# Sliding-window attention inside the projection stage: other start slots for its steps, other slots for the K and V turns, and another order in the sample stage

## What is computed

```python
z = rms_norm(x, norm_g) @ w_in                      # q, k, v, gate | wq, wk, wv, wgate
# stick-breaking, per head
log_keep = where(mask, log_sigmoid(-z), 0)
after = cumsum(log_keep, reverse=True) - log_keep
o = where(mask, exp(log_sigmoid(z) + after), 0) @ v
# sliding window: own chunk of 64 and the 128 frames before it, ALiBi distance, a learned sink
s = q @ k.T * HEAD_DIM ** -0.5 - slope * dist
m = maximum(max(s), sink)
o = (exp(s - m) / (sum(exp(s - m)) + exp(sink - m))) @ v
y = x + concat(o_sb * silu(g_sb), o_win * silu(g_win)) @ w_out
```

## Time and profile before

| | us |
|---|---|
| median of 3 runs | 1626.79 (1624.41 to 1630.45) |
| the profiled execution, device time | 1632.45 |
| its span, first to last instruction | 1630.60 |
| PE busy | 1458.9 (89%) |
| DVE busy | 1034.8 (63%) |
| ACT busy | 905.9 (56%) |
| POOL busy | 598.1 (37%) |
| mean granted TensorE clock | 0.945 of 2.4 GHz |

### The profile page before, as it was taken

One profiled execution on the slowest core, in us unless ns is written; L12 is line 12 of the kernel. 1 busy time (PEld: TensorE's weight loads), 2 busy tenths in 40 slices (PEclk: granted clock), 3 DMA queues, 4 the chain that ended last, 5 costly groups with the idle time before them and its releaser, 6 DMA issues. The chain is left out here.

```text
span 1630.6 us, 23640 instructions
## 1 busy us (share of the span) xinstructions
PE 1458.9 (89%) x7794; PEld 1217.1 (75%) x7794; DVE 1034.8 (63%) x1446; ACT 905.9 (56%) x1922; POOL 598.1 (37%) x497
## 2 busy tenths in 40 slices
PE   3698997999998898896799899989999998999989
PEld 2576785777777777775799789967888777877767
DVE  5355541656655655753467776678878799888841
ACT  7322222454543544452477666667777787777731
POOL 1010012120110120110455864557565677565742
PEclk9798897999898999997799999999999999999999
DMA  5034424443343342334587867666475555434533
GB/s 209 27 142 150 153 66 153 129 127 111 107 126 114 108 142 85 118 124 137 141 267 223 232 196 225 185 189 193 151 216 173 171 177 177 120 117 143 180 120 104
DMA packets 257981, 245.79 MB, mean 151 GB/s; under 512 B 21472, under 2 KB 190296, under 8 KB 257096
## 3 DMA queue, kind: packets, MB, share of 16 engines
q1 hardware_dynamic: 257864, 244.32, 49.4%
HBM read 163.74 MB, written 80.71 MB: 150 GB/s over the span
## 5 line engine op out<-in xcount | busy, mean ns | idle before, releaser
L1318 POOL TENSOR_TENSOR c_weight<-cache_k_rows,f_kept 128x512 f32<-128x512 f32 (+2 forms) x320 | 306.4, 984 | 91.7 <-PE c_turn L1501 79.3
L1424 DVE TENSOR_TENSOR_SCAN f_kept<-f_keep,f_kept,c_score 128x513 f32<-128x513 f32 x192 | 245.2, 1277 | 44.3 <-ACT cache_k_rows L1346 37.2
L1432 DVE TENSOR_TENSOR c_w_lo<-c_turn,c_w_hi 128x512 fp32r<-128x512 f32 (+1 forms) x320 | 191.9, 600 | 79.7 <-ACT c_w_hi L1354 76.8
L1354 ACT ACTIVATE c_w_hi<-c_turn 128x512 fp32r<-128x512 f32 (+1 forms) x320 | 171.4, 536 | 127.8 <-PE c_turn L1501 124.4
L1096 POOL TENSOR_TENSOR f_w_lo<-f_w_raw,f_w_hi 128x1024 fp32r<-128x1024 f32 x64 | 154.0, 2407 | 200.6 <-ACT f_w_hi L1092 200.5
L871 PE MATMUL b_ps<-XH,w_w_hi 128*128 128x512 f32 (+1 forms) x480 | 191.0, 398 | 6.6 <-DVE b_vwin L822 6.6
L1346 ACT ACTIVATE cache_k_rows<-c_score 128x512 f32<-128x512 f32 (+2 forms) x320 | 173.1, 541 | 31.7 <-POOL c_weight L1318 31.5
L873 PE MATMUL b_ps<-XH,w_w_lo 128*128 128x512 f32 (+1 forms) x480 | 184.0, 384 | 0.0
L872 PE MATMUL b_ps<-XL,w_w_hi 128*128 128x512 f32 (+1 forms) x480 | 183.9, 383 | 0.0
L1501 PE MATMUL c_turn<-ident,c_weight 128*128 128x128 f32 x1088 | 172.4, 274 | 4.9 <-POOL c_weight L1318 3.0
L1343 ACT ACTIVATE f_keep<-c_score 128x512 f32<-128x512 f32 (+2 forms) x320 | 171.1, 535 | 10.0 <-PE c_score L1492 5.2
(11 more groups left out here) (227 smaller groups left out, 3251.6 us busy)
## 6 DMA issues: line engine op xcount, KB each, us to landing
f_k<-k_parts SPq DMA_DIRECT2D x80, 256.0 KB, 4.1
f_v<-v_parts SPq DMA_DIRECT2D x80, 256.0 KB, 2.7
f_q<-q_parts SPq DMA_DIRECT2D x64, 256.0 KB, 5.1
f_w_raw<-in_w_in SPq DMA_DIRECT2D x32, 512.0 KB, 4.1
f_w_raw<-in_w_out SPq DMA_DIRECT2D x32, 512.0 KB, 4.4
w_w_raw<-in_w_in SPq DMA_DIRECT2D x18, 512.0 KB, 5.3
x_rows<-in_x_prompt SPq DMA_DIRECT2D x4, 2048.0 KB, 10.1
b_qraw<-normT SPq DMA_DIRECT2D x32, 256.0 KB, 3.9
```

The lines of the kernel that those rows point to most:

```text
L1318: pool.tensor_tensor(weight[:, u.number % 2, j, 0:n], take[:, j, 0:n], kept[:, j, 1:n + 1], ALU.mult).then_inc(weighted, 1)
L1354: act.activation(w_hi[n][:, cols], turn_ps[c % 2][:, cols], ACT.Copy).then_inc(hi_ready, 1)
L1424: dve.tensor_tensor_scan(kept[:, j, down], keep[:, c % 2, down], score[c % 2][:, 0:1].to_broadcast([P, n]), above, ALU.mult, ALU.bypass).t ...
L1432: dve.tensor_tensor(w_lo[n][:, cols], turn_ps[c % 2][:, cols], f32(w_hi[n][:, cols]), ALU.subtract).then_inc(lo_ready, 1)
```

## The change

In the pair stage the steps begin at slots 8, 22, 37, 52, 67, ... (8 + floor(59 st / 4)) up to 465, which is a pitch of 14, 15, 15, 15 in turn; the lags of the first turn, second turn and second mix become 12, 14 and 17; K and V groups are turned at 5 slots behind their end and stored at 7; PE no longer waits for `start_done` ahead of its first triple. In the stick-breaking stage the loads for block 1 begin at slot 12 with two slots between them, where they began at 2 with three. In the sample stage PE takes the stick-breaking scores ahead of the three sliding turns, and turns `take` ahead of the sliding scores; DVE adds the mask and does both scans first, then copies `win` out, then does the sliding softmax.

```diff
@@ pair_project_stage
-        PERIOD, OFFSET = 14, 16
+        OFFSET = 8
+        BEGIN = [OFFSET + 59 * st // 4 for st in range(STEPS)]
@@ step_at
-            st, r = divmod(x - lag - OFFSET, PERIOD)
-            return st if r == 0 and 0 <= st < STEPS else None
+            return BEGIN.index(x - lag) if x - lag in BEGIN else None
@@
-        SOFTEN, EXP, SPLIT, NORM, Q_LO, TURN0, TURN1, MIX1 = 0, 4, 5, 6, 8, 10, 13, 16
-        TURN_LAG, STORE_LAG = 3, 6
+        SOFTEN, EXP, SPLIT, NORM, Q_LO, TURN0, TURN1, MIX1 = 0, 4, 5, 6, 8, 12, 14, 17
+        TURN_LAG, STORE_LAG = 5, 7
@@ pair_project_stage, tensor
-            pe.wait_ge(start_done, 1)
@@ x_pieces
-                    begin = 2 if b == 1 else [p for p in gates if p.b == b - 1][-1].end() + 1
-                    out += [(b, dt) for dt in range(DT) if c == begin + 3 * dt]
+                    begin = 12 if b == 1 else [p for p in gates if p.b == b - 1][-1].end() + 1
+                    out += [(b, dt) for dt in range(DT) if c == begin + (2 if b == 1 else 3) * dt]
@@ sample_stage, vector
+            dve.wait_ge(mask_ready, 1)
+            dve.wait_ge(scored, 2)
+            for g in range(2):
+                dve.tensor_tensor(znew[:, g], z_new[:, g * NS:(g + 1) * NS], mask[:], ALU.add).then_inc(znew_ready, 1)
+
+            def scan(g):
...
+            dve.wait_ge(cleared, 1)
+            for g in range(2):
+                scan(g)
             dve.wait_ge(win_turned, 1)
...
-            dve.wait_ge(mask_ready, 1)
-            dve.wait_ge(scored, 2)
-            for g in range(2):
-                dve.tensor_tensor(znew[:, g], z_new[:, g * NS:(g + 1) * NS], mask[:], ALU.add).then_inc(znew_ready, 1)
...
                 dve.tensor_tensor(sink_in[:, gc], shift[:, gc], sink[:, gc], ALU.add).then_inc(step, 1)
-                scan(g)
@@ sample_stage, tensor
-            pe.wait_ge(w_in, 6 * 16)
-            pe.transpose(win[:, 0:P], wk_rows[:], s.ident[:])
-            pe.transpose(win[:, P:2 * P], wkT_last[:], s.ident[:])
-            pe.transpose(win[0:NS, 2 * P:3 * P], wkT[:, WINDOW:], s.ident[:]).then_inc(win_turned, 1)
             pe.wait_ge(kT_ready, 4)
...
                 last.then_inc(scored, 1)
-            pe.wait_ge(win_ready, 3)
-
-            pe.wait_ge(znew_ready, 2)
-            for g in range(KV):
-                col = P + g * (WINDOW + NS)
-                pe.matmul(z_new[:, col:col + WINDOW + NS], wq[:, g], wkT[:], start=True, stop=True).then_inc(win_scored, 1)
+            pe.wait_ge(w_in, 6 * 16)
+            pe.transpose(win[:, 0:P], wk_rows[:], s.ident[:])
+            pe.transpose(win[:, P:2 * P], wkT_last[:], s.ident[:])
+            pe.transpose(win[0:NS, 2 * P:3 * P], wkT[:, WINDOW:], s.ident[:]).then_inc(win_turned, 1)
             for g in range(2):
                 pe.wait_ge(weighted, g + 1)
...
+            pe.wait_ge(win_ready, 3)
+
+            pe.wait_ge(znew_ready, 2)
+            for g in range(KV):
+                col = P + g * (WINDOW + NS)
+                pe.matmul(z_new[:, col:col + WINDOW + NS], wq[:, g], wkT[:], start=True, stop=True).then_inc(win_scored, 1)
```

More of the change, by code:

```diff
@@ L1705, in _ @@
                 dve.tensor_copy(kT[:, c, 0:PAST], turn[c][:]).then_inc(kT_ready, 1)
+            dve.wait_ge(mask_ready, 1)
[3 more added lines that the diff above has]
+            def scan(g):
+                dve.wait_ge(take_ready, 2 * g + 2)
+                dve.tensor_scalar(keep[:, g], take[:, g], -1.0, 1.0, ALU.mult, ALU.add).then_inc(keep_ready, 1)
+                dve.wait_ge(keep_ready, g + 1)
+                dve.tensor_tensor_scan(kept[:, g, NK - 1::-1], keep[:, g, ::-1], keep[:, g, ::-1], 1.0,
+                                       ALU.mult, ALU.bypass).then_inc(scanned, 1)
+            dve.wait_ge(cleared, 1)
+            for g in range(2):
+                scan(g)
             dve.wait_ge(win_turned, 1)
@@ L1722, in _ @@
             dve.wait_ge(dist_ready, 3)
[L1724 to L1731, removed]
             for g in range(KV):
@@ L1791, in _ @@
                 last.then_inc(scored, 1)
+            pe.wait_ge(w_in, 6 * 16)
+            pe.transpose(win[:, 0:P], wk_rows[:], s.ident[:])
+            pe.transpose(win[:, P:2 * P], wkT_last[:], s.ident[:])
+            pe.transpose(win[0:NS, 2 * P:3 * P], wkT[:, WINDOW:], s.ident[:]).then_inc(win_turned, 1)
+            for g in range(2):
+                pe.wait_ge(weighted, g + 1)
+                for b in range(PB):
+                    pe.transpose(turn[g][:, b * P:(b + 1) * P], take[:, g, b * P:(b + 1) * P], s.ident[:])
+                pe.transpose(turn[2 + g][0:NS, 0:P], take[:, g, PAST:], s.ident[:]).then_inc(w_turned, 1)
             pe.wait_ge(win_ready, 3)
@@ L1797, in _ @@
                 pe.matmul(z_new[:, col:col + WINDOW + NS], wq[:, g], wkT[:], start=True, stop=True).then_inc(win_scored, 1)
[L1798 to L1802, removed]
             pe.wait_ge(prob_ready, 3)
```

## The result

The changed kernel is slower: 1646.7 us (median of 4 runs, 1645.0 to 1650.8) against 1626.7 (4 runs), a ratio of 1.0124 with a 95% interval of 1.0097 to 1.0152. Forecast were 1624 us and a range up to 1640; the time lies outside, beside the slower rival's 1645.

The account below looks back on a forecast made before the run. PE was taken to bound the last stage, with the pair stage losing 43.7 us in waits and about 37 in clock. Pair stage -1.2 and sample stage -1.6 gave -2.8 us from 1626.8, so 1624 us, range 1602 to 1640.

Parts of the forecast that it names:

- slower rival: Pair stage: late copies show whole behind two triples of cover, five more than summed, 21 us lost, 1645 us; chance 0.19.
- First turns: Pair stage, first turns of probabilities at lag 12 instead of 10: waits fall from 28.6 to 8 us, 20.6 us won.
- Second mixes at pitch 14: Pair stage: at eight steps DVE's softmax runs ahead of the low-part copy; 17 us of waits, 1 us at other second mixes.
- First mixes: Pair stage, two triples instead of three between the turns: new waits at first mixes 13 us, bounds 9 and 18.
- 5 us more: Pair stage, first mixes: ACT's late copies behind `empty`, no longer covered by the third triple, add 5 us of wait.
- Half clock: Pair stage: 11 or 12 half-clock stretches against 11, each behind a wait of 1.46 us or more; 0, 3.1 us per stretch.
- K and V turns: Pair stage, turns at lag 5 instead of 3: waits fall from 7.6 to 1.2 us, 6.4 us won.
- Ends of the stage: Pair stage: first triple 0.9 us sooner without the wait for DVE's clearing; longer tail after the last triple, 3.2 us lost.
- Sample stage: Sample stage: scores no longer wait for the sliding loads, mask 5.0 us sooner, later chain longer; 1.6 us won.
- Loads for block 1: Last stage: later issue of these loads stays covered by 14 us of PE's work; 0.
- faster rival: Pair stage: second mixes wait with few half-clock stretches, 1605 us, or DVE isn't late at all, 1588 us; chance of both 0.32.
- frequent short waits cool the clock: Pair stage: about 25 waits of 0.25 us ahead of first mixes each bring 3.1 us, near 1700 us; chance 0.02.

Follow-up runs that it names:

- e1: The changed kernel with DVE's copies of the turned probabilities ahead of the next step's softmax in a slot; 1637.7 us, 1.0048 of the kernel before.
- e8: The changed kernel with SP's store of a step's output and the value block's load three slots later; 1634.2 us, 1.0019 of the kernel before.
- d1: The changed kernel with only the store of a step's output three slots later, the value block's load unmoved; 1633.2 us, 1.0019 of the kernel before.
- e2: The kernel before with the change to the sample stage alone; 1632.5 us, 1.0017 of the kernel before.
- e3: The kernel before with the change to the pair stage alone; 1654.9 us, 1.0144 of the kernel before.
- d3: The kernel before with only the store of a step's output moved to 4 slots behind the second mix; 1618.9 us, 0.9939 of the kernel before.
- e4: The kernel before with only K and V groups turned at 5 and stored at 7 slots behind their end; 1630.8 us, 1.0008 of the kernel before.
- c3: The kernel before with the store of a step's output and the value block's load three slots later; 1618.9 us, 0.9927 of the kernel before.
- d4: The changed kernel with DVE's copies ahead of the softmax and the output store late, value block's load left early; 1613.2 us, 0.9897 of the kernel before.

## Why the prediction was wrong, step by step

**First turns: right.** Forecast 20.6 us won, measured 19.9.

**Second mixes at pitch 14: right.** Forecast 17 us for eight steps and 1 for others. Measured 14.6 us at the eight (1.83, 1.77, 1.34, 0.96, 0, 3.27, 2.28, 3.14) and 17.3 in all; e1 removed 12.5 of them by DVE's order alone.

**First mixes: the step that failed.** The sum had 7.7 us of short waits and "5 us more" for late copies, 13 in all. Measured were 23.5: 5.3 of short waits, and 18.2 at six late ones. The two behind the end of a K group make 4.9, just what the term held; the 13.3 us at the four behind a late store are what it lacked. The 5 us were taken from the mixes' waits of before, and those are what was left over behind a cover of three triples; the lateness itself, which the trace of before did show, as ACT's and DVE's waits for their own stores, wasn't read (waits of ACT in the pair stage of the kernel before):

```profile
ACT b_part L683 <- DMA q_parts<-b_part: 11.7, 4, 3.5
...
ACT b_rows L699 <- DMA out_sb_v_prompt<-b_rows: 8.1, 3, 2.8
```

The cause ahead of it is SP's order, and the prediction looked at SP's queue only for what was moved past it. With that order mended (e8) the changed kernel's first mixes wait 14.0 us, with the store alone moved (d1) 10.3, near the sum's 13. The stage then takes 482.4 us from the first triple on, with 11 stretches. In that count the forecast was -0.3 us (-1.2 without the 0.9 at the start) and 11 or 12 stretches, that is 485.4 us from the profile of before or 481.7 from e2's: with this one cause out of the way the sum for the stage nearly holds. Of the 15.6 us by which the stage missed the forecast in the two profiles (start included), 10.5 are first mixes, 3.9 the clock, 1.4 the first scores and 1.2 the tail; these add up to some 1 us too much, within what single profiles can tell.

**Half clock: wrong, and its premise with it.** Forecast 0, with 3.1 us for each stretch more. Measured: six more stretches, and 7.7 us more of PE's work in them (66.1 to 73.8), which costs the half of that, 3.9 us, or 0.65 for each stretch more: several are shorter than those of before and hold more waiting. (Between e2 and e3, the same two pair stages again, it is 59 to 75 us of work at half clock, 8 us of cost, so the size of this term is known only to a factor of two; it isn't 0 in either pair, and under 3.1 for each stretch in both.) The premise was that a wait of 1.46 us or more, and nothing else, brings such a stretch. The trace of before had hardly a row against it (only at 590 us had the clock fallen by the moment the wait began, behind narrow triples). The changed kernel has several, two of them seen in its busy time by stretch (columns as in the earlier trace rows):

```profile
349.00:351.00 2.00, 2.00 (x13) 1.69 (x12) 1.39 (x4) 0.60 (x1) 0.00 (x0) 1.00 0.99 280
351.00:353.00 2.00, 0.60 (x3) 0.16 (x1) 1.90 (x5) 0.00 (x0) 0.00 (x0) 1.00 0.58 172
353.00:357.00 4.00, 3.62 (x16) 2.95 (x17) 0.96 (x2) 2.68 (x10) 0.00 (x0) 1.00 0.06 16
...
676.00:680.00 4.00, 4.00 (x34) 3.83 (x32) 3.85 (x9) 3.20 (x8) 0.00 (x0) 0.99 0.01 2
680.00:683.00 3.00, 3.00 (x8) 2.39 (x8) 2.87 (x6) 1.42 (x8) 0.00 (x0) 0.50 0.56 196
```

A wait of 1.77 us at 353 has no half clock behind it, and at 680 the clock falls with PE busy all the time, behind eight narrow triples with one mix and four transposes among them. Of the 17 stretches 11 have a wait of 1.7 us or more at their head; six begin in or behind narrow triples, with waits of 1.11 us or less or none. (The prediction's use of the Trainium skill, "TensorE: Matmul & The Clock Gate", section "Terms", stands: d3's pair stage had 24 us less at half clock, of which PE worked in 22, and its busy time fell by 10.9 us, a half of that.)

**K and V turns: the size right, the worth wrong.** 6.4 us forecast, 6.7 measured at those turns. But e4 shows that alone they bring nothing: 7.4 us came off them and 7.6 went on at the mixes. The sum booked the term as if it were on its own.

**Ends of the stage.** First triple 0.9 us sooner, as forecast. The tail is 4.3 us longer, forecast 3.2: PE was at half clock there (a mix took 0.77 us, not 0.39), and ahead of the last mix it waited 1.0 us. Not forecast: 1.4 us ahead of the first scores (L902 in the waits above), since `b_klo` wasn't ready at a start 8 slots sooner.

**Sample stage: right in the two profiles.** Forecast 1.6 us won, measured 2.3; mask 5.3 us sooner (forecast 5.0). That both profiles fell on the shorter level of this stage was luck; e2 alone won nothing in the time. **Loads for block 1: about right.** The last stage took 836.9 us instead of 835.5; over all profiles it is 833.5 to 836.6 with the old order of loads and 835.2 to 839.0 with the new one, 1 us more in the mean.

**The rivals.** The slower one came true in its mechanism and nearly in its number: it asked for five late copies more than in the sum, at 1.2 us of wait and 3.1 of clock each. What came was four more than the two that the sum's 5 us could hold, with 3.3 us of wait each and at most some 1 us of clock, so near that the number owes something to luck. Against it the prediction had said that "most of these steps have their group's end elsewhere"; but the queue of SP hands the delay on from a group's end to copies several slots behind. It had a chance of 0.19, and the range stopped 5 us short of its time, though the text gave a condition ("from about three") that a count of ACT's waits for stores could have weighed. The faster rival is refuted for this change: DVE did come late, in seven of the eight steps. That frequent short waits cool the clock is refuted at this spacing: its 1700 us didn't come, and the many waits of 0.06 to 0.12 us at first mixes, shorter than the 0.25 it spoke of, have no stretch of their own.

**Open.** Why the late store in the kernel before takes 24 us of half clock out of the pair stage's profile, with the first turns' waits unchanged at 29 us, is not settled: the waits at mixes fall by 4 us only. Part of it is the draw of single executions: e2's profile has the same pair stage as before with 70 us at half clock instead of 76. The mean granted clocks of all runs, over the whole kernel, show 169 us (d3) and 167 us (c3) at half clock against 174 in the kernel before, so how much of the usual gain is clock stays open; that the store is worth 0.6 to 0.7% doesn't hang on it. That the phase of waits against narrow triples matters would fit, but no run moves the narrow triples alone. The two first mixes behind a K group's end were left as they are: no run moves those copies.

## What to carry to other kernels

Before a gap between a producer and its consumer is made shorter, don't price it by the consumer's waits of before, which are what is left behind the cover; read how late the producer already is, and follow that back through every in-order queue, the one that issues the DMAs above all. A store that waits for the newest result belongs behind the stores that free a buffer: moving one issue by three slots was worth 0.6 to 0.7% here, the K and V lags alone nothing. And a wait removed at one place is won only if the next one on the same path has slack: measure such terms alone before they are added up. And where two versions share a stage word for word, use their profiles as repeats of it: here they showed that single profiles of the pair stage differ by up to 4 us.

## What was not expected of the hardware

- PE's clock fell to half behind runs of 32-column matmuls with no wait at all (0.99 to 0.50 at 680 us in the changed kernel, PE busy for 4.00 of 4.00 us ahead of it, a mix and four transposes among the narrow ones), and stayed up through a wait of 1.77 us at 353. In d4 all five stretches ahead of the last triple have a wait of 2.1 us or more at their head, and none of the eleven narrow groups ahead of the last brought one alone. So narrow triples don't always do it, and no run shows what decides.
- Time at half clock was worth as much as waits or more in the profiles: of the 12.2 to 15.9 us that the late store won in the pair stage of the kernel before, 7.9 to 10.9 were PE's busy time, with the same instructions. The clocks of all the runs show less of it (see "Open").
- The store of `q_parts` issued at 615.93 let its waiter go at 620.29, 4.4 us later, behind five loads issued just ahead of it; the median of the 16 such stores is 2.8 us (DMA issues of the changed kernel: transfer, count, KB each, median us to landing). In this stage the 14 stores of parts and of K and V rows that follow the block loads took 3.0 to 4.4 us to land; the others have medians of 2.8 us (parts) and 2.3 us (rows). So the queued loads seem to delay the store twice, in its issue and in its landing; the second was not tried by itself.

```profile
q_parts<-b_part SPq DMA_DIRECT2D x16, 512.0 KB, 2.8
```
